# Two transformer blocks with mixtures of experts on one core: weight loads and constant matmuls rearranged around the routers and the layer boundary

## The reference, cut to what matters

```python
x = first_block(x, ...)                  # three mixers, gated FFN, norm; 512 tokens of width 1024
for i in range(2):                       # second block, two layers
    mod = silu(c) @ ada_w[i] + ada_b[i]; sh1, sc1, g1, sh2, sc2, g2 = split(mod)
    h = rms_norm(x, norm1_g[i]) * (1 + sc1) + sh1
    y = diff_attention(h, ...) if i == 0 else stick_breaking_attention(h, ...)
    x = x + g1 * y
    h = rms_norm(x, norm2_g[i]) * (1 + sc2) + sh2
    y = hierarchical_moe(h, ...)         # top group of 4, top 2 of its 8 experts; 32 experts, 1024 -> 512 -> 1024
    x = x + g2 * y
return rms_norm(x, final_norm_g)
```

## Time and profile before

| | us |
|---|---|
| median of three runs (2566.26 to 2567.08) | 2567.02 |
| profiled execution, device time | 2569.1 |
| its span | 2567.3 |
| TensorE busy, share of the span | 2229.0, 87% |
| 16 DMA engines: mean rate | 229 GB/s |

### The profile page before, as it was taken

One profiled execution on the slowest core, in us unless ns is written; L12 is line 12 of the kernel. 1 busy time (PEld: TensorE's weight loads), 2 busy tenths in 40 slices (PEclk: granted clock), 3 DMA queues, 4 the chain that ended last, 5 costly groups with the idle time before them and its releaser, 6 DMA issues. The chain is left out here.

```text
span 2567.3 us, 21848 instructions
## 1 busy us (share of the span) xinstructions
PE 2229.0 (87%) x8414; PEld 997.5 (39%) x8414; DVE 614.2 (24%) x1326; ACT 457.0 (18%) x830; POOL 263.2 (10%) x508
## 2 busy tenths in 40 slices
PE   8999999999999998868877778599899688877775
PEld 4454454444444445443322222244454433222222
DVE  1364522112002019241001101220273410010004
ACT  2323310000002017110000000110394110000001
POOL 3121120000000002111111111000021011111110
PEclk9999999999999999869989999899999799999998
DMA  7478725112211102058999999910003579999995
GB/s 254 172 243 292 283 94 214 41 55 104 89 66 66 66 36 96 33 203 342 428 427 428 426 417 409 348 55 14 33 1 123 213 279 426 427 428 427 424 421 237
DMA packets 128018, 586.69 MB, mean 229 GB/s; under 512 B 17896, under 2 KB 29552, under 8 KB 103372
## 3 DMA queue, kind: packets, MB, share of 16 engines
q1 hardware_dynamic: 112480, 548.72, 53.6%
q0 software_dynamic: 14864, 36.76, 3.8%
q10 hardware_dynamic: 604, 0.27, 0.0%
HBM read 571.31 MB, written 30.65 MB: 234 GB/s over the span
## 5 line engine op out<-in xcount | busy, mean ns | idle before, releaser
L226 PE MATMUL ps<-hT,ring 128*128 128x512 f32 (+3 forms) x1328 | 560.5, 584 | 4.2 <-issue 4.2
L1836 PE MATMUL ps<-ring,arena 128*64 128x512 f32 x1952 | 464.0, 624 | 114.9 <-DMA ring<-in_expert_w_up 62.4
L226 PEld LDWEIGHTS ps<-hT,ring 128*128 128x128 f32 (+1 forms) x1328 | 249.2, 190 | 313.7 <-issue 309.9
L1836 PEld LDWEIGHTS ps<-ring,arena 128*64 128x64 f32 x1952 | 145.7, 143 | 403.2 <-issue 294.3
L1869 PE MATMUL ps<-ring,arena 128*64 128x512 f32 x1024 | 242.1, 628 | 64.8 <-DMA ring<-in_expert_w_down 33.8
L233 PE MATMUL ps<-ring,hT 128*128 128x512 f32 x576 | 252.3, 597 | 3.6 <-ACT hT L194 1.6
L233 PEld LDWEIGHTS ps<-ring,hT 128*128 128x128 f32 x576 | 109.2, 192 | 136.6 <-issue 133.5
L1869 PEld LDWEIGHTS ps<-ring,arena 128*64 128x64 f32 x1024 | 81.5, 144 | 203.3 <-issue 186.4
L1909 DVE TENSOR_TENSOR arena<-ps,arena 128x512 f32<-128x512 f32 x32 | 22.1, 692 | 548.1 <-PE ps L1836 548.1
L1070 PE MATMUL ps<-ring,arena 128*128 128x512 f32 x336 | 144.8, 592 | 0.8 <-issue 0.8
L1914 DVE TENSOR_TENSOR arena<-ps,arena 128x1024 f32<-128x1024 f32 x30 | 36.7, 1225 | 296.9 <-PE ps L1869 296.9
(11 more groups left out here) (361 smaller groups left out, 2066.5 us busy)
## 6 DMA issues: line engine op xcount, KB each, us to landing
ring<-in_expert_w_down SPq DMA_DIRECT2D x64, 2048.0 KB, 17.5
ring<-in_expert_w_up SPq DMA_DIRECT2D x62, 2048.0 KB, 17.4
ring<-in_expert_w_gate SPq DMA_DIRECT2D x60, 2048.0 KB, 17.0
ring<-in_ada_w SPq DMA_DIRECT2D x24, 2048.0 KB, 12.3
ring<-in_diff_w_in SPq DMA_DIRECT2D x6, 2048.0 KB, 8.4
ring<-in_sb_w_in SPq DMA_DIRECT2D x6, 2048.0 KB, 19.6
ring<-in_ffn_w_gate SPq DMA_DIRECT2D x5, 2048.0 KB, 14.8
ring<-in_ffn_w_val SPq DMA_DIRECT2D x5, 2048.0 KB, 14.0
```

The source lines that it names most:

```text
L226: mm = pe.matmul(out, w[:, c, cols], x[:, c, :], start=(c == 0), stop=(c == chunks - 1))
L1836: mm = pe.matmul(k.ps[slots, 2 + kind, :], k.xT[:, c, slots], w[:, c, :], start=(c == 0), stop=(c == KD - 1))
```

## The change

In layer 1 the attention weights begin at slot 0 and attention's working data is in slots 3 to 5. All eight pieces of them are issued in the second part. Three pairs instead of two use the nine places in turn before the loop, and a fourth is written out. The last tile is transposed before the logits of the tile before it. At three places of each router TensorE multiplies constants (`keep_clock`: identity by ones, 128 columns, 10, 26 and 28 matmuls), whose result nobody reads. In layer 0's tail two of the four `placed` products move behind the transposes of tile 0 and tile 1; in layer 1's tail, tile 3's stored rows are added by TensorE with diagonal matrices (`last_diag`) and not by VectorE. The diff, cut to its core:

```diff
-def qkv_tensor(pe, k, a, turns):
+def qkv_tensor(pe, k, a, turns, besides={}):
     for j in range(QKV_JOBS):
         if j in turns:
             turn_tensor(pe, k, a.norm, turns[j])
+        if j in besides:
+            besides[j]()
...
+def keep_clock(pe, k, bank, n):
+    for _ in range(n):
+        pe.matmul(k.ps[:, bank, 0:P], k.ident[:, :], k.ones[:, :], start=True, stop=True)
...
 def out_proj_tensor(pe, k, a, m):
...
+    hT_ready(pe, m.norm, TT - 2)
+    keep_clock(pe, k, 3, 10)
+    turn_tensor(pe, k, m.norm, TT - 1)
     logits_tensor(pe, k, m, TT - 2)
-    turn_tensor(pe, k, m.norm, TT - 1)
     logits_tensor(pe, k, m, TT - 1)
+    keep_clock(pe, k, 7, 26)
...
 def router_tensor(pe, k, m):
...
     mm.then_inc(m.ranked, 1)
+    keep_clock(pe, k, 7, 28)
...
 def moe_places(k, pair):
     ring = [k.ring[:, slot, :] for slot in range(RING)]
-    if pair == 0:
-        return ring[0:2], ring[2:4], ring[4:6]
     if pair == 1:
-        return [k.spare[0], k.spare[1]], [k.spare[2], ring[0]], ring[1:3]
-    return ring[3:5], [ring[5], ring[0]], ring[1:3]
+        return k.spare[0:2], [k.spare[2], ring[0]], ring[1:3]
+    if pair == 2:
+        return ring[3:5], [ring[5], k.spare[0]], k.spare[1:3]
+    return ring[0:2], ring[2:4], ring[4:6]
...
 def moe_sync(sp, k, m, a, t):      # from pair 2's first gate on; gate(p, b), up, down: load it
...
     sp.wait_ge(m.downed, 2)
-    weights(m.w_gate, gates[1], 5, m.gate_landed)
-    weights(m.w_up, ups[0], 4, m.up_landed)
+    gate(2, 1, m.gate_landed)
+    up(2, 0, m.up_landed)
+    sp.wait_ge(m.gated, 3)
+    up(2, 1, m.up_landed)
+    down(2, 0, m.down_landed)
     sp.wait_ge(m.upped, 3)
-    weights(m.w_up, ups[1], 5, m.up_landed)
+    down(2, 1, m.down_landed)
+    gate(3, 0, m.gate1_landed)
     sp.wait_ge(m.downed, 3)
-    for b in range(2):
-        weights(m.w_down, downs[b], 4 + b, m.down_landed)
+    gate(3, 1, m.gate1_landed)
+    up(3, 0, m.up1_landed)
+    sp.wait_ge(m.gated, 4)
+    up(3, 1, m.up1_landed)
+    down(3, 0, m.down1_landed)
+    sp.wait_ge(m.upped, 4)
+    down(3, 1, m.down1_landed)
...
 def last_slots_vector(dve, k, m, ch, last):
...
+    for c in range(2):
+        weight = k.weights[:, c * TT + TT - 1:c * TT + TT]
+        done = ch.mark(dve.tensor_scalar(k.last_diag[:, c, :], k.ident[:, :], weight, None, ALU.mult))
...
+def placed_tensor(pe, k, t, cb, tt, whole=False):
+    if whole:
+        pe.wait_ge(t.loaded[tt], 16)
+    for half in range(2):
+        cols = slice(half * 512, (half + 1) * 512)
+        out = k.ps[:, 2 * tt + half, :]
+        mm = pe.matmul(out, k.last_hot[:, tt, :], k.ys[:, cols], start=True, stop=not whole)
+        for c in range(2 * whole):
+            mm = pe.matmul(out, k.last_diag[:, c, :], k.yg[:, 2 * tt + c, cols], start=False, stop=(c == 1))
+    mm.then_inc(cb.placed, 1)
...
 # first part, SP
-            last = moe_sync(sp, k, m, a, k.tails[0])
-            sp.wait_ge(m.gated, last + 2)
-            for n in range(2):
-                k.stream2.load(sp, n)
-            sp.wait_ge(m.upped, last + 2)
-            for n in range(2, 4):
-                k.stream2.load(sp, n)
+            moe_sync(sp, k, m, a, k.tails[0])
...
 # second part, SP
-            sp.wait_ge(first.halves, 2)
-            for n in range(4, 8):
+            for n in range(8):
+                if n == 4:
+                    sp.wait_ge(first.halves, 2)
                 a.stream.load(sp, n)
...
 # second part, TensorE
-            last_results_tensor(pe, k, k.tails[0], first)
-            qkv_tensor(pe, k, a, {0: 0, 1: 1, 3: 2, 5: 3})
+            last_results_tensor(pe, k, t, first)
+            for tt in range(2):
+                placed_tensor(pe, k, t, first, tt)
+            qkv_tensor(pe, k, a, {0: 0, 1: 1, 3: 2, 5: 3}, {j: lambda tt=j + 2: placed_tensor(pe, k, t, first, tt) for j in range(2)})
...
             last_results_tensor(pe, k, k.tails[1], last)
+            for tt in range(TT):
+                placed_tensor(pe, k, k.tails[1], last, tt, whole=(tt == TT - 1))
...
 # second part, VectorE, both tails; below it the last tail only
-            combine_vector(dve, k, t, last, 1)
+            combine_vector(dve, k, t, last, 1, (0,))
             last_results_vector(dve, k, last, 1)
+            combine_vector(dve, k, t, last, 1, (1,))
             for tt in range(TT):
                 placed_vector(dve, k, last, tt)
-                if tt + 2 < TT:
-                    combine_vector(dve, k, t, last, tt + 2)
+                if tt == 0:
+                    combine_vector(dve, k, t, last, 2)
```

More of the change, by code:

```diff
@@ L47 @@
 NOWHERE = 4095.0
-TURN = 3
 RING = 6
@@ L1424 @@
 SB_W = 1280
-SB_LENT = 3
+SB_LENT = RING - 3
 SB_AHEAD = 4
@@ L1753, in weights, with gate, up, down @@
         sp.dma_start(dst, src).then_inc(landed, 16)
-    late = [a.stream.slot(a.first_piece + 6 + half) for half in range(2)]
-    gates, ups, downs = moe_places(k, 0)
+    def gate(pair, b, landed):
+        weights(m.w_gate, moe_places(k, pair)[0][b], 2 * pair + b, landed)
+    def up(pair, b, landed):
+        weights(m.w_up, moe_places(k, pair)[1][b], 2 * pair + b, landed)
+    def down(pair, b, landed):
+        weights(m.w_down, moe_places(k, pair)[2][b], 2 * pair + b, landed)
+    late = [(a.first_piece + 6 + half) % RING for half in range(2)]
     sp.wait_ge(a.proj, QKV_JOBS)
-    lent = range(SB_LENT) if a.lends else ()
+    lent = range(SB_LENT, RING) if a.lends else ()
     for slot in sorted(range(RING), key=lambda n: (n in late, n in lent)):
@@ L1764, in moe_sync @@
         if slot < 2:
-            weights(m.w_gate, gates[slot], slot, m.gate_landed)
+            gate(0, slot, m.gate_landed)
         elif slot < 4:
-            weights(m.w_up, ups[slot - 2], slot - 2, m.up_landed)
+            up(0, slot - 2, m.up_landed)
         else:
-            weights(m.w_down, downs[slot - 4], slot - 4, m.down_landed)
-    gates, ups, downs = moe_places(k, 1)
+            down(0, slot - 4, m.down_landed)
     sp.wait_ge(a.x_ready, TT)
-    weights(m.w_gate, gates[0], 2, m.gate1_landed)
+    gate(1, 0, m.gate1_landed)
@@ L1774, in moe_sync @@
     sp.wait_ge(m.logits, TT)
-    weights(m.w_gate, gates[1], 3, m.gate1_landed)
+    gate(1, 1, m.gate1_landed)
     sp.wait_ge(m.rows_stored, 16 * (TT - 1))
     sp.wait_ge(t.y_stored, 16)
-    weights(m.w_up, ups[0], 2, m.up1_landed)
+    up(1, 0, m.up1_landed)
     sp.wait_ge(m.gated, 2)
-    weights(m.w_up, ups[1], 3, m.up1_landed)
-    weights(m.w_down, downs[0], 2, m.down1_landed)
+    up(1, 1, m.up1_landed)
+    down(1, 0, m.down1_landed)
     sp.wait_ge(m.upped, 2)
-    weights(m.w_down, downs[1], 3, m.down1_landed)
@@ L1785, in moe_sync @@
-    gates, ups, downs = moe_places(k, 2)
-    weights(m.w_gate, gates[0], 4, m.gate_landed)
+    down(1, 1, m.down1_landed)
+    gate(2, 0, m.gate_landed)
     sp.wait_ge(m.downed, 2)
-    weights(m.w_gate, gates[1], 5, m.gate_landed)
-    weights(m.w_up, ups[0], 4, m.up_landed)
+    gate(2, 1, m.gate_landed)
[3 more added lines that the diff above has]
+    down(2, 0, m.down_landed)
     sp.wait_ge(m.upped, 3)
-    weights(m.w_up, ups[1], 5, m.up_landed)
+    down(2, 1, m.down_landed)
@@ L1808, in moe_sync @@
     last = last_pair(sp, k, m)
-    with sp.Fori(0, last - 3) as i:
-        later(i + 3, m.down_landed)
-    later(last, t.down_landed)
+    with sp.Fori(0, last - 4) as i:
+        later(i + 4, m.gate_landed, m.up_landed, m.down_landed)
+    later(last, m.gate1_landed, m.up1_landed, t.down_landed)
     sp.wait_ge(t.y_stored, last * 16 + 16)
```

58 lines of the change are left out of this document (27 added, 31 removed).

## The result

The changed kernel takes 2526.94 us (median of 4 runs, 2525.57 to 2529.47); the kernel before, beside it, 2567.05 (2566.26 to 2572.42). The ratio is 0.984, 95% interval 0.9823 to 0.9858. The prediction was 2523 with a range of 2509 to 2539.

The account below looks back on a forecast made before the run. The DMA stream was taken to bound the experts, so its start and holes count. Gains of 8.0 + 5.3 + 16.2 + 7.0 + 4.6 + 2.7 = 43.8 us off the median 2567.0 gave 2523, range 2509 to 2539.

Parts of the forecast that it names:

- The boundary: Between the layers: without SP's four attention issues TensorE starts 17.3 us earlier; with 0.7 won and 1.8 added, net 16.2.
- The doubt about the weights' landing: Behind the boundary: with a landing time of 21.8 us the first attention piece would cost 3.2 us; taken as 0.
- so both holes go: 5.3 + 4.6: Second pair's stretch: nine places for three pairs remove empty DMA time, 5.3 us in layer 0, 4.6 in layer 1.
- Layer 0's router: Up to T0, when the first pair's gates are multiplied: new order and constants bring T0 8.0 us earlier.
- seven matmuls at 0.44: Router's 26 constants: seven at low clock, 19 at 0.22, 7.4 us in all, so the ranks start 1.1 late.
- Layer 1's router: T0 7.0 us earlier: as layer 0's 8.0, less 1 us for GpSimd's wait for the gain's load.
- The tail: Last tail: 1.3 us from moving tile 1's second add, 1.4 from dropping tile 3's two adds; sum 2.7.
- A: Rival, routers: the constants don't lift the clock, T0 7.9 us later than before in each layer, 2554; 6%.
- B: Rival, boundary: the barrier waits for something else than SP and the 16.2 us don't come, 2539; 6%.
- C: Rival, places: the holes stay because the stream is short of free places all the same, 9.9 less, 2533; 8%.
- D: Rival: clock up from first constants to first gates and at the boundary, 3 us more per router and 1.7, 2515; 13%.
- E: Rival: the stream, now without holes, runs at a lower rate; at 411 GB/s throughout 33 us are lost, 2556; 4%.

Follow-up runs that it names:

- the single edit: The kernel before, with only SP's loads of attention pieces 0 to 3 moved behind the barrier: 2550.23 us, ratio 0.9931.
- the dose of two pieces: The changed kernel with attention pieces 0 and 1 issued again ahead of the barrier: 2535.63 us, ratio 0.9878.
- five constants: The kernel of both together, with five constant matmuls more behind the last hidden multiply of each layer: 2514.76 us, ratio 0.9795.
- the places alone: The changed kernel with routers, boundary and tails as before, so only the places of the weights differ: 2555.61 us, ratio 0.9951.
- the wait moved: The changed kernel with GpSimd's wait for the final norm's gain moved behind layer 1's first gather: 2522.38 us, ratio 0.9817.
- both together: The changed kernel with GpSimd's wait for the gain behind the first gather and 10 and 6 more constants around the table of weights: 2520.21 us, ratio 0.9813.
- the tail alone: The kernel before with only the two tails' edits (last_diag, three-matmul product for the last tile, new order of adds): 2567.34 us, ratio 0.9994.

## Why the prediction was right, and where not

**The boundary, right.** Predicted 17.3 - 1.1, measured 17.5 - 2.3. "All engines left the second barrier 2.3 later" was the mechanism; the single edit, and the dose of two pieces, showed that SP's issues alone set it. The doubt about the weights' landing (3.2 us) didn't come true: the first piece landed in 13.4 us and not in 21.8. What fell short is 0.7 us said to be won before the first attention matmul: it was -0.4, as the clock fell at 1608.8, in TensorE's idle time ahead of the downs, and these took 9.98. I had counted "no gain there (up to 1.7)"; five constants show that it was worth 2.9. The move of two products behind the transposes won nothing by the prediction's own count (+0.7 - 1.8), and no run has it alone: against the boundary alone, downs to the issue of layer 1 took 2.3 us more, 1.2 of it in the slower downs (9.98 against 8.78).

**The places, right in kind and undersized.** Predicted 5.3 and 4.6, alone 6.8 and 5.0, in the changed kernel 7.7 and 5.9. So the step "so both holes go: 5.3 + 4.6" had its size wrong: it took only the 20 us of the earlier trace rows, and empty DMA time lies in more than that. Over the 80 us behind T0 the rates differ by (413 - 380) and (417 - 384) GB/s, and 80 x 33 / 427 = 6.2 us in either layer. What remains in layer 0, 1.5, fits a slow spell that was shallower in this execution, 418 GB/s instead of the 411 of the earlier trace rows (over 110 us 1.8), and with the places alone it was less, 6.8. So that part is likely chance and not the change; no run isolated it.

**Layer 0's router, right in sum by two errors.** Predicted 8.0, measured 7.7. Less the inherited 2.5 us, the ranks came 6.9 earlier (predicted 6.9 - 1.1 = 5.8), the first table 8.1 (7.2), the gather 8.9 (8.0). The term "seven matmuls at 0.44" was wrong here: the clock was never low between the first constants and the table, transposes and logits included. What I left out lies behind: the clock fell at 1131.0, in the 2.45 us gap ahead of the second table, which has no constants, and stayed at half until 1144.6. Before, it had come up at 1153.6, 3.2 us into the first gates; now 5.5 us of them ran at half, they took 9.86 us instead of 8.70, and from gather to T0 1.3 were given back. Sixteen more constants there brought T0 3.6 us earlier. That the sum came out at 7.7 is luck: the error of 1.1 and the 1.3 left out cancel.

What stood behind the term was the earlier trace rows, a stretch busy 4.00 of 4.00 us at 0.50. 3.3 of those 4.00 us are logits (L1596, 1111.68 to 1115.28), and without the constants a stretch of logits alone was busy 4.00 of 4.00 us at 0.50. So narrow logits alone went with a clock that stayed at half. Tile 3's transposes ran in 1.16 us at the full clock with constants just before them and in 1.97 at half without the constants; no run has transposes alone. That the stretch lets the clock go was my estimate: behind the first constants the same transposes and logits went at 1.00, from 1108.00 to 1113.00. The term's price, 1.1 us, was not lost in layer 0.

**Layer 1's router, the step that failed.** Predicted 7.0, got 3.9. The prediction had the mechanism, "GpSimd waits for the gain's load first", and mis-sized its term: 1 us. The gain landed in 24.4 us instead of the earlier trace rows's 20.8, and the gather started 0.8 behind that, so it went 31.7 us behind the issue; with the wait moved it went at 27.4. I had set the landing against a fixed 20.8 and allowed 1 us, and an earlier gather leaves the same load less time. The landing hangs on the router's order: in the four profiles with the old one it took 18.9 to 22.0 us, in the ten with the new one 23.8 to 24.6. In the new order the last two prefetches are issued sooner behind the gain (1.6 and 7.1 us after it, before 8.2 and 8.7); that these slow it is likely, and no run isolated it. The 26 constants, same code as in layer 0, took 7.44 us here, because the clock fell at 1991.1, and made the ranks about 0.8 late; that cost nothing, since the gain came later. With the wait moved the 5.2 us come.

**The tail, mis-sized.** Predicted 2.7, got 0.8. Of its two terms, 1.4 for tile 3's adds came: one interval fell from 5.7 to 4.3, and from the first `placed` to the end 26.5 became 25.2. The 1.3 for tile 1's second add was eaten by the downs ahead, 8.78 instead of 7.09 because the clock was at half from 2489.5 to 2492.9; VectorE waited 1.55 for them, and from the last hidden multiply to `placed` it took 12.8 instead of 12.2. With the downs at the full clock (both together) that was 11.0, a gain of 1.2. The prediction's sum for the tail had no term for the clock there. Where it was up, last hidden to the end gained 2.5 (both together) and 3.4 (the tail alone).

**The rivals.** A, constants that don't lift the clock: no, 52 records in 6.05 us. B, another wait at the barrier: no. C, holes remain: no. D, the clock up throughout: true up to the table in layer 0, not beyond, and not at the boundary; the last experiment makes D true in layer 0 and at the boundary, not in layer 1, where the clock was at half from 1986.8 to 1993.6, within the logits and the 26 constants. That it came to 2514.8, next to D's 2515, is chance, as it has the gain's wait moved as well. E, a slower stream: no. The spell of the earlier trace rows is there in each of six kernels whose stream I cut in stretches of 50 and 60 us, from 1480 to 1540 us at 408 to 416 GB/s, wherever T0 lay; in a seventh, the whole change without its constants, the same stretch moved 420. Its next 50 us differ, 413 to 426. It makes 2 to 3 us between executions, not 33. Its cause is open. (The prediction's "at 389 it would be 2601" doesn't follow from its own numbers: 900 x (426 / 389 - 1) = 86, so 2609.)

Errors of both signs (-3.1 in layer 1's router, -1.9 in the tail, -1.2 behind the barrier, +3.7 for the places) left 41.1 of 43.8. That the whole came so close is in part luck.

## What to carry to other kernels

Look at who is last at a barrier before looking at what it was doing it for: issues that hold their engine make an early prefetch cost the whole time that they hold it, here 18 us, and loading after the barrier cost nothing. A load that is hidden now comes out when the work before it gets shorter: its slack is its landing time in the new traffic, not in the old (here the gain's 24.4 us, not 20.8). Constant matmuls paid here only in front of work that is on the path, and up to the next wide matmuls: in layer 0 the three sets of constants brought 4.3 us, and covering the last two gaps 3.6 more; in layer 1 they brought nothing as long as a load held the gather.

## What was not expected of the hardware

The issues of 2 MB attention pieces held SP for 10.58 us for two and 25.76 for six. Of the six the first took 0.59, the second 4.03 and the others 5.1 to 5.3 each; expert weights of the same size were issued in 0.7 us at most, mostly in 0.33 to 0.38, also with others still under way. No run shows what makes the difference. The gain of 0.5 MB on GpSimd's queue took 24.4 us to land beside 2 MB prefetches, 20.8 before.

The same constants behind the same transposes and logits kept the full clock in layer 0, and in layer 1 lost it for 3.4 us, with the engine busy throughout. This is the stretch of the kernel after in layer 1:

```profile
1990.00:1994.50 4.50, 4.50 (x27) 4.50 (x27) 2.31 (x11) 0.67 (x2) 0.77 (x2) 0.63 0.99 409
```

It made the constants 1.4 us longer (7.44 instead of 6.05). It is no accident of one execution: in all eight profiles with these constants the 26 took 6.05 us in layer 0 and 7.4 to 8.9 us in layer 1. Why one layer and not the other is open, and no run isolated it.
